# Prompt attention of a hybrid decoder step: query rows on partitions in the outputs, one norm for all heads, units in five slots

## The reference, cut to what matters

```python
def diff_attn_core(q, k, v, q_pos, k_pos, lam):
    s = einsum('bqhd,bkhd->bhqk', q, k) * HEAD_DIM ** -0.5      # 16 half-heads of 64
    s = where(k_pos <= q_pos, s, NEG_INF)
    p = softmax(s).reshape(b, N_HEADS, 2, lq, lk)               # 8 heads, 2 halves each
    a = p[:, :, 0] - lam * p[:, :, 1]
    return einsum('bhqk,bkhe->bqhe', a, v)                      # 128 values per head

# finish_layer
oa = rms_norm(o_attn, attn_subln) * (1 - lambda_init)           # over the 128 values of a head
x = x + concatenate([oa, c_out]) @ w_out
h = rms_norm(x, mlp_norm) @ w_up
x = x + square(relu(h)) @ w_down
```

## Time and profile before

| what | before |
| --- | --- |
| median of 3 runs | 1704.58 us (1700.35 to 1705.51) |
| the profiled execution | 1703.94 us |
| its span, first to last instruction | 1702.2 us |
| granted clock of TensorE, mean | 0.943 |
| PE busy | 1550.0 us (91%) |
| DVE busy | 988.1 us (58%) |
| ACT busy | 620.5 us (36%) |
| POOL busy | 420.7 us (25%) |
| DMA | 340.50 MB, mean 200 GB/s |

### The profile page before, as it was taken

The page is one execution under the profiler, slowest core; times in us unless marked ns, Lnnn a source line. Parts: engine busy times, 40 slices in busy tenths (PEclk is TensorE's granted clock), DMA queues, the critical chain, the costliest instruction groups (busy, mean ns, idle before and its releaser), DMA issues.

```text
span 1702.2 us, 32371 instructions
## 1 busy us (share of the span) xinstructions
PE 1550.0 (91%) x11299; PEld 1381.3 (81%) x11299; DVE 988.1 (58%) x1483; ACT 620.5 (36%) x948; POOL 420.7 (25%) x654
## 2 busy tenths in 40 slices
PE   6999887898887877779999999999999999999998
PEld 4988765565565544439999999999999999999998
DVE  3587756998998575524455454455445454445444
ACT  4433222122123344414354433344334343344433
POOL 4893546756776444100000000000000000000000
PEclk9999999988988777779999999999999999999999
DMA  6746689999999565564445544555545555455453
GB/s 180 230 129 179 206 287 333 348 310 318 346 314 353 157 195 184 158 237 135 150 149 162 166 166 162 170 162 166 168 162 168 163 165 167 161 167 165 163 169 130
DMA packets 163844, 340.50 MB, mean 200 GB/s; under 512 B 33915, under 2 KB 33971, under 8 KB 163168
## 3 DMA queue, kind: packets, MB, share of 16 engines
q1 hardware_dynamic: 120592, 267.29, 48.8%
q0 software_dynamic: 43168, 72.15, 13.8%
HBM read 334.00 MB, written 5.96 MB: 200 GB/s over the span
## 4 chain that ended last, share of the span: by engine, by line
PE 75%; DVE 8%; issue 6%; DMA 6%; ACT 3%; POOL 1%; POOLq 1%; SPq 0%; ACTq 0%; DVEq 0%
PE acc L586 21%; PE acc L588 21%; PE acc L587 21%; DMA v_page<-in_cache_v 3%; DMA k_page<-in_cache_k 2%; DVE conv L1468 2%; PE aux L659 2%; PE acc L808 1%; DVE w_lo L1330 1%; DVE k_page L1402 1%; PE aux L683 1%; PE aux L717 1%; PE acc L604 1%; PE acc L830 1%; POOL k_page L493 1%
## 5 line engine op out<-in xcount | busy, mean ns | idle before, releaser
L1330 DVE TENSOR_TENSOR w_lo<-raw,w_hi 128x1024 fp32r<-128x1024 f32 x368 | 451.0, 1226 | 523.3 <-ACT w_hi L989 522.4
L989 ACT CAST w_hi<-raw 128x1024 fp32r<-128x1024 f32 x368 | 385.9, 1049 | 723.0 <-PE acc L588 723.0
L586 PE MATMUL acc<-a_hi,w_hi 128*128 128x288 f32 (+1 forms) x1920 | 593.4, 309 | 35.1 <-DVE w_lo L1330 23.2
L587 PE MATMUL acc<-a_lo,w_hi 128*128 128x288 f32 (+1 forms) x1920 | 580.0, 302 | 0.0
L588 PE MATMUL acc<-a_hi,w_lo 128*128 128x288 f32 (+1 forms) x1920 | 579.8, 302 | 0.0
L586 PEld LDWEIGHTS acc<-a_hi,w_hi 128*128 128x128 f32 x1920 | 369.7, 193 | 80.0 <-issue 43.7
L493 POOL DMA_DIRECT2D k_page<-in_cache_k x512 | 332.2, 649 | 257.0 <-PE aux L659 134.1
L587 PEld LDWEIGHTS acc<-a_lo,w_hi 128*128 128x128 f32 x1920 | 370.2, 193 | 0.5
L588 PEld LDWEIGHTS acc<-a_hi,w_lo 128*128 128x128 f32 x1920 | 370.1, 193 | 0.0
L588 PE MATMUL acc<-h_hi,w_lo 128*128 128x288 f32 x1024 | 302.2, 295 | 0.0
L587 PE MATMUL acc<-h_lo,w_hi 128*128 128x288 f32 x1024 | 301.5, 294 | 0.0
(11 more groups left out here) (217 smaller groups left out, 1006.3 us busy)
## 6 DMA issues: line engine op xcount, KB each, us to landing
k_page<-in_cache_k POOLq DMA_DIRECT2D x512, 128.0 KB, 6.2
v_page<-in_cache_v SPq DMA_DIRECT2D x128, 512.0 KB, 8.3
raw<-in_w_up SPq DMA_DIRECT2D x128, 512.0 KB, 3.7
raw<-in_w_down SPq DMA_DIRECT2D x128, 512.0 KB, 3.7
raw<-in_w_in SPq DMA_DIRECT2D x80, 512.0 KB, 5.6
raw<-in_w_out SPq DMA_DIRECT2D x32, 512.0 KB, 3.7
x_nat<-in_x_prompt SPq DMA_DIRECT2D x3, 1024.0 KB, 9.0
out<-y_nat SPq DMA_DIRECT2D x8, 256.0 KB, 2.7
```

The lines of the kernel that those rows point to most:

```text
L586: mm(out, wh, ah, start=(kt == 0), stop=False)
L587: mm(out, wh, al, start=False, stop=False)
L989: nc.scalar.copy(w_hi[:, j % SPL], raw[:, j % RAW]).then_inc(hi_ok, 1)
L1330: v.tensor_tensor(w_lo[:, j % SPL], raw[:, j % RAW], w_hi[:, j % SPL].bitcast(F32), ALU.subtract)\
```

## The change

Every unit is spread over five slots, in a software pipeline that runs across the two bodies and into the last: p_score in slot 2u, maximum and exp in 2u+1, difference in 2u+2, transposes and copies in 2u+3, output and its copy in 2u+4. `prob`, `pstat` have two buffers. p_score reads q in `z` directly, with the 64 rows of each half, and p_out reads v in `v_nat` directly; the staged copies are gone. p_out has its operands exchanged, so that its result has queries on partitions; the copy in `z` holds that. The difference is made without normalizing (a row is p1 - lambda (l1/l2) p2, with l1 and l2 the sums of exps), and ACT's square of a unit gives its sum of squares per query. In the last body one factor per query and unit is made for all 16 units at once, DVE scales the units, PE transposes them (`turn_heads`), and ACT copies them out with the gain (`keep_head`).

In these bodies decode scores stand at slots 0, 4, 8, 12 in place of 3, 7, 11, 15, pages are transposed four slots ahead in place of two (two more before the first of the bodies), and the maxima at slots 2, 6, 10, 14, so that the whole maximum comes in slot 15.

```diff
+FREE_SCORES = {SG * g: g for g in range(NG)}
+FREE_MAXES = {SG * g + 2: g for g in range(NG)}
+FREE_TURNS = {j: j + SG for j in range(N_PAGES)}
+UNITS = 2 * N_H
 # PE
-            def p_score(u, h, blk):
-                pe.wait_ge(sq_ok, 2 * (h + 1))
-                pe.wait_ge(pa_exp, 1 + 2 * u)
+            def p_score(u):
+                if u:
+                    pe.wait_ge(pa_exp, 2 * u)
 ...
-                        mm(acc[:, i, k0:k1], q_st[:, i, P * blk:P * (blk + 1)],
-                           z[:, ds(8 + h, 1), PAD + k0:PAD + k1]...)
+                        mm(out[:, k0:k1], heads_at(u)[rows], z[rows, 8 + h, PAD + k0:PAD + k1], ...)
+            def p_turn(u):
+                pe.wait_ge(pa_v, 3 * (u + 1))
+                if u:
+                    pe.wait_ge(pa_tc, 2 * u)
+            def p_out(u):
+                pe.wait_ge(pa_tc, 2 * (u + 1))
 ...
-                    last = mm(acc[:, 3, 0:P], v_st[0:n, i, :], probT[0:n, i, :],
+                    last = mm(acc[:, 3, 0:P], probT[0:n, i, :], v_nat[0:n, i + 1, P * h:P * (h + 1)],
-            def sub_sum(h):
-                pe.wait_ge(sub_sq, h + 1)
-                mm(acc[:, 3, P:3 * P], ones[:], sq_st, start=True, stop=True).then_inc(sub_mm, 1)
+            def prompt_middle(slot):
+                if slot % 2 and 0 <= slot - 3 < 2 * UNITS:
+                    p_turn((slot - 3) // 2)
+                if slot % 2 == 0 and 0 <= slot - 4 < 2 * UNITS:
+                    p_out((slot - 4) // 2)
+            def turn_heads(j):
+                if j == 5:
+                    pe.wait_ge(of_v, 1 + UNITS)
+                    for h in range(MT):
+                        turn_head(h)
+                if j == 8:
+                    for h in range(MT, N_H):
+                        pe.wait_ge(sub_v, h - MT + 1)
+                        turn_head(h)
 # ACT
+            def p_exp(u):
+                if u >= 2:
+                    act.wait_ge(pa_t, u - 1)
 ...
+            def p_square(u):
+                act.wait_ge(pa_oc, u + 1)
+                fn(sq_st, heads_at(u), ACT.Square, accum_out=o_sq[:, u:u + 1]).then_inc(sub_sq, 1)
+            def attend(slot):
+                if slot % 2:
+                    if slot < 2 * UNITS:
+                        p_exp(slot // 2)
+                    if slot >= 3:
+                        p_copy((slot - 3) // 2)
+                elif slot >= 4:
+                    p_square((slot - 4) // 2)
+                if j == 4:                          # last body
+                    act.wait_ge(of_ok, 2)
+                    fn(o_fac[:], o_fac[:], ACT.Sqrt, scale=1.0 / P).then_inc(of_rt, 1)
+                if j in (6, 9):
+                    ... keep_head(h)                # four heads each
-                if j == 2:
+                if j == 4:
 ...
+                    act.wait_ge(pa_o, UNITS)
                     for c in range(8):
                         nc.scalar.copy(a_hi[:, 8 + c, 0:T_OUT], conv[:, c, :])...
 # DVE
+            turn(N_PAGES * (PAIR_V + 1) + LEAD)
+            turn(N_PAGES * (PAIR_V + 1) + LEAD + 1)
             go_on(work, CONV_S * TAPS)
+            def p_diff(u):
+                dve.wait_ge(pa_exp, 2 * (u + 1))
+                v.reciprocal(coef[:, 0:1], l_stat[:, u, 1:2])
+                v.scalar_tensor_tensor(coef[:, 1:2], l_stat[:, u, 0:1], neg_lam[:, 0:1], coef[:, 0:1], ...)
+                v.scalar_tensor_tensor(p1, p2, coef[:, 1:2], p1, ALU.mult, ALU.add)
+            def attend(slot):
+                if slot % 2 == 0:
+                    if slot >= 2:
+                        p_diff((slot - 2) // 2)
+                    if slot >= 4:
+                        p_take((slot - 4) // 2)
+                if j == 4:                          # last body
+                    dve.wait_ge(sub_sq, UNITS)
+                    ... o_fac = l1 * l1 * EPS * P + o_sq, root by ACT, reciprocal
+                    for u in range(UNITS):
+                        v.tensor_scalar(heads_at(u), heads_at(u), o_fac[:, u:u + 1], None, ALU.mult)
```

More of the change, by code:

```diff
@@ L283, in build_step @@
         sub_mm = sem("sub_mm")
+        of_ok = sem("of_ok")
+        of_rt = sem("of_rt")
+        of_v = sem("of_v")
+        of_t = sem("of_t")
         sub_rt = sem("sub_rt")
@@ L816, in p_turn @@
[L816 to L820, removed]
-                last.then_inc(pa_t, 1)
[L823 to L828, removed]
+                        mm(out[:, k0:k1], heads_at(u)[rows], z[rows, 8 + h, PAD + k0:PAD + k1], start=True, stop=(k0 == 0))
@@ new lines, in p_score, with key_tiles @@
+                    mm(out[:, nk - P:nk], ident[:], causal, start=False, stop=True).then_inc(pa_s, 1)
+            def key_tiles(u):
+                return [(0, P), (P, P), (2 * P, N_META)] if u % 2 else [(0, P), (P, N_META)]
+            def p_turn(u):
+                pe.wait_ge(pa_v, 3 * (u + 1))
+                if u:
+                    pe.wait_ge(pa_tc, 2 * u)
+                for i, (k0, n) in enumerate(key_tiles(u)):
+                    last = transpose(acc[0:n, 2, P * i:P * (i + 1)], prob[:, u % 2, 0, k0:k0 + n], ident[:])
+                last.then_inc(pa_t, 1)
@@ L856, in _, with turn_head @@
             for s in range(ATT_S, ATT_S + 2):
[L857 to L863, removed]
-                        p_turn(u0 + j // 2 - 1, (j // 2 - 1) % 2)
-                        if j % 4 == 2 and j > 2:
-                            sub_sum(h0 + j // 4 - 1)
-                    elif j % 2 and j > 1:
-                        out(j // 2 - 1)
-                    elif j == N_PAGES:
-                        out(N_PAGES // 2 - 1)
+                slot0 = N_PAGES * (s - ATT_S)
                 def end(j):
-                    k = j // 2
                     if j % 2 == 0:
-                        p_score(u0 + k, h0 + k // 2, k % 2)
-                    elif j == N_PAGES - 1:
-                        p_turn(u0 + k, k % 2)
+                        p_score((slot0 + j) // 2)
                     if s == ATT_S:
                         layer_sums(j)
-                body(s + 1, s, None, middle, end, finish=lambda: sub_sum(h0 + HB - 1))
+                body(s + 1, s, None, lambda j: prompt_middle(slot0 + j), end, scores=FREE_SCORES)
+            def turn_heads(j):
[7 more added lines that the diff above has]
+                        turn_head(h)
+            def turn_head(h):
+                for u in (2 * h, 2 * h + 1):
+                    last = transpose(acc[:, h % MT, P * (u % 2):P * (u % 2 + 1)], heads_at(u), ident[:])
+                last.then_inc(of_t, 1)
             def new_values(j):
@@ L1473, in go_on, with body @@
                     next(work, None)
-            def body(ks, vs, n, beside=None, finish=None, first=False, turns=TURNS, maxes=MAXES):
+            def body(ks, vs, n, beside=None, finish=None, first=False, turns=TURNS, maxes=MAXES, before=None):
                 def group(g):
@@ L1515, in body @@
                             lo(n + 1, 0)
+                    if ks is not None and maxes is FREE_MAXES and j == N_PAGES - 1:
+                        whole_max()
                     if beside:
@@ L1519, in body @@
                     beside(N_PAGES)
-                if ks is not None:
+                if ks is not None and maxes is not FREE_MAXES:
                     group(NG - 1)
-                    dve.wait_ge(sn_a, ks + 1)
-                    v.tensor_reduce(s_max[:, NG:NG + 1], s_rows[:, PAST:PAST + N_SMP], AX, ALU.max).then_inc(s_mx, 1)
-                    dve.wait_ge(s_mx, (NG + 1) * (ks + 1))
-                    v.tensor_reduce(neg_max[:], s_max[:], AX, ALU.max, negate=True).then_inc(nm_ok, 1)
+                    whole_max()
                 if vs is not None:
```

215 lines of the change are left out of this document (96 added, 119 removed).

## The result

The kernel after takes 1663.25 us (median of 4 runs, 1659.43 to 1665.41), the kernel before beside it 1705.05 us (4 runs, 1700.35 to 1709.47): a ratio of 0.976, interval 0.9732 to 0.9787. The profiled execution took 1663.14 us, its span is 1661.2 us. The forecast was 1666.

A forecast was written before the change was run, and what follows sets the result against it. The two passes were taken as bound by a chain stepped through unit by unit, not any engine's work; -23 (waits) -7 (summing matmuls) -12 (clock) +4 (last pass) = -38 us on 1703.94 gave 1666 us, range 1645 to 1690.

The forecast's parts named there:

- What would show it: Signs in the two passes: difference wait under 3 us, only layer-norm table loads, clock near 0.87, about 129 us.
- New idle time of 18 us in place of 41: PE in the two passes: start 3, layer norm 8, p_out 6, smaller waits 1; -23 us.
- the 39 us: PE's waits in the passes, 32.2 us for the difference and 6.9 for staged q, expected to go with five slots.
- my first rival: In the passes the chain forms again on ACT and DVE, 1.5 us a unit, 24 us lost: 1690 us, chance 0.12.
- No summing matmuls: -7: In the passes sub_sum's 16 records, 7.0 us of PE, leave and nothing covers PE: -7 us.
- The form of p_score: 0, at most 3.5 either way: In the passes, as many matmuls with half the rows: 0, bounds half of sub_sum's 7 us either side.
- Work off DVE and ACT counted at nothing: Reciprocals, scalings, roots, table loads and copies leave the passes; neither engine sets the pace, so 0 by itself.
- The clock: -12: In the passes the slow share of PE's work falls from 0.40 to 0.2: -12 us, bounds 0 and -24.
- The last pass: +4: PE waits for scaled heads and the pause stops page loads: +4 us, bounds -3 to +9.
- The loads: nothing: Page loads in the passes land in time: 0, up to 18 us in all if landings went to several times that.
- The rule of short waits: Many short idle times between matmul groups can make the clock go back and forth; the -12 us becomes 0 or a loss.

The follow-up runs named there:

- e10: Kernel after with units over two slots, decode work at its old slots and a unit's maxima behind the page turn, removed work still away: 1702.29 us, ratio 1.0006.
- e13: Kernel after, units still over five slots, with decode work at its old slots and a unit's maxima behind the page turn: 1687.88 us, ratio 0.9911.
- e9: Kernel after with units over two slots and unused roots, reciprocals, scalings and first products of p_diff put back in the chain: 1682.45 us, ratio 0.9917.
- e5: Kernel after with the staged, zero-padded q copies back, so p_score multiplies over 128 rows in place of 64: 1653.35 us, ratio 0.9729.
- e2: Kernel after with unused square roots on ACT and reciprocals on DVE put back, seven of each, off PE's path: 1676.43 us, ratio 0.9846.
- e3: Kernel after with unused matmuls added ahead of TensorE's three long waits in the passes: 1654.82 us, ratio 0.9723.
- e1: Kernel after with units over two slots again, its arithmetic, decode schedule and last pass kept: 1666.62 us, ratio 0.9801.

## Why the prediction was right, and where it was not

The number was right: 1666 forecast, 1663.25 measured, and the passes in the state that "What would show it" asked for: no wait for the difference, the layer norm's table loads alone, a clock of 0.87, 133.1 us for the 129. Passes and last pass together gave 36.3 us of the 38; another 4.7 us lie ahead of and behind them, in no term of the sum. That the number came out so near is in part luck, as the steps show:

- *New idle time of 18 us in place of 41.* 21.5 us measured. The start cost 4.0 for 3, the layer norm 7.9 for 8. p_out's waits were 2.1 us, not 6. The boundary of the passes, 3.4 us, is in no term: I did not ask what stands on DVE's queue behind the wait for ACT's exps, now that a score group heads the next pass.
- *Who removed the waits.* I gave the 39 us to the five slots alone. The waits for the difference do go with them (20.5 us in e10, 1.6 in e13), but with the old order waits for ACT's copies come in their place, 18.6 us, and the idle time falls most of the way without the five slots (e10, e9). e13 is the mechanism of my first rival (the chain forms again on ACT and DVE). Its 1690 us are near the 1687.88 measured, but by luck: I had priced it as 24 us of waits, and against after the idle time grew by 0.8 us and PE's busy time by 15.0. It did not come true in the kernel after because the change also put the maxima ahead of the page turns and moved the decode work, edits to which the prediction gave next to nothing and which are worth 26 us.
- *No summing matmuls: -7.* Not tested by itself. *The form of p_score: 0, at most 3.5 either way.* Mis-sized: 10.3 us of PE work, 7.4 us of the passes (e5). I had taken half the rows to be no dearer.
- *Work off DVE and ACT counted at nothing.* Failed: 12 us of the passes (e2), 8.5 of them in the first pass, though neither engine was short of time (DVE busy for 96 and ACT for 62 of 145 us). I had named the place where the cover ends, DVE's queue at the layer norm, but took its price to be the 8 us already counted. The wait grew by only 1.07 us and the idle time not at all; the lower clock made the 12 us.
- *The clock: -12.* The mean of 0.87 was right. PE's busy time fell by 18.8 us where my -7 and -12 make 19; but with the dearer p_score in it, the clock gave, by my estimate, some 22 (18.8 - 7 + 10.3), not 12. Two errors of 10 us cancelled. e3 shows that some 7 us more were to be had. And my reading that the slow stretches stand behind waits of 2.9 to 8 us was too narrow for the trace it was taken from. Kernel before:

```profile
632.41 0.64 PE L820 MATMUL acc<-ident,prob 128*128 128x128 f32 x3 [1.47 <-DVE prob L1641]
635.53 1.91 PE L717 MATMUL aux<-v_page,pT 128*16 128x256 f32 x16
```

  Two pages take 1.91 us behind a wait of 1.47 us, 0.96 each, as behind the 2.88 us of the earlier trace rows.
- *The last pass: +4.* +2.2 measured; the wait for the scaled heads was 0.5 us, so the pages and `new_values` did cover them, and the loads were waited for less than before. What made the pass longer is PE's own work, 29.3 us for 23.8, where I had looked for a wait.
- *The loads: nothing.* Right: no wait for key pages' DMA, at a share of 0.69 for the 0.73 forecast.
- *The rule of short waits* (the Trainium skill, "TensorE: Matmul & The Clock Gate", section "A second HAM failure mode: psum-queue depth-cycling"), which I set aside by the earlier trace rows: with the new order the trace stayed with the rows (e1, 655 to 670 us: 1.00 with waits up to 1.03 us). In e10 something like it happened, as a low clock for most of the second pass (0.57 on average); but there the waits were few and 1.2 to 2.8 us long, not many and short.

## What to carry to other kernels

When a wait is ended by an engine whose queue holds other work, try first to put the waiting work ahead of that other work: here this was worth 26 to 35 us, more slots of slack 7 to 16. Read the clock beside the idle time and do not price waits by their length alone: with the same 25 us of idle time TensorE was busy for 36 us more in one arrangement than in another. Work taken off an engine that is not the bound can still pay: put back, it cost 12 us of the passes without any more idle time.

## What the runs showed of the hardware that was not expected

- The low clock level can hold for some 15 us while TensorE is busy all the time (e2, 605 to 620 us) or all but 0.13 us of it (e10, 680 to 695 us, 0.50, after a wait of 1.27 us), and be gone 4 us after a wait of 7.94 us (after, 606.90 us). It can also come in the midst of work: in the kernel after the wait between the passes ends at 621.47 us, the clock comes back (a group of four products at 626.32 us takes 0.66 us, at 630.47 us 1.06), and it falls again while PE is busy without a break:

```profile
625.00:630.00 5.00, 5.00 (x30) 3.82 (x27) 1.84 (x5) 2.10 (x8) 3.44 (x6) 0.84 0.42 116
630.00:635.00 5.00, 5.00 (x25) 3.34 (x24) 3.95 (x11) 0.89 (x3) 4.29 (x7) 0.50 0.53 151
```

  Waits of up to 1.6 us in the paired stage left it at 1.00. Neither the length of the wait alone nor busy time decides; what does, these runs leave open.
- Matmuls over 64 rows between matmuls over 128 rows cost 0.14 us a change at full clock (0.57 us for four), worked out from the two fences under e5. Halving the rows saved nothing: the first group of products takes 0.73 us in both forms.
